# Up projections and gates: the high weights times both parts of the rows in one 512-column product, the halves added by VectorE

## The reference, cut to what matters

```python
# first block
proj = n @ w_in[l]                      # columns for q, k, v of two attentions, then the gates ga, gb
gate_a = sigmoid(ga + b_gate[l, :D_MODEL]);  gate_b = sigmoid(gb + b_gate[l, D_MODEL:])
h = h + (gate_a * ya + gate_b * yb) @ w_out[l]
...
u = n @ w_up                            # conv_gated_mlp: 1024 -> 2 * 2816, gate half and value half
u = causal_depthwise_conv3(u) + conv_b
h = h + (silu(u[..., :D_FF]) * u[..., D_FF:]) @ w_down
# second block, layer 0
x = x + (silu(h @ wg) * (h @ wu)) @ wd  # ffn_wg_2, ffn_wu_2: 1024 -> 2816 each
# second block, layer 1: top-2-of-8 expert SwiGLU, then a final rms_norm
```

## Time and profile before

| | |
|---|---|
| median of 3 runs | 1805.52 us (1805.26 to 1806.93) |
| the profiled execution, its own time | 1807.05 us |
| its span in the profile | 1805.3 us (25215 instructions) |
| PE busy | 1738.2 us (96%) |
| PE weight loads busy | 1425.7 us (79%) |
| DVE busy | 1184.4 us (66%) |
| ACT busy | 915.0 us (51%) |
| POOL busy | 55.9 us (3%) |
| DMA | 495.14 MB, mean 274 GB/s |
| chain that ended last | PE 81%, DVE 10%, ACT 6%, issue 2% |

### The profile page before, as it was taken

One profiled execution on the slowest core, in us unless ns is written; L12 is line 12 of the kernel. 1 busy time (PEld: TensorE's weight loads), 2 busy tenths in 40 slices (PEclk: granted clock), 3 DMA queues, 4 the chain that ended last, 5 costly groups with the idle time before them and its releaser, 6 DMA issues.

```text
span 1805.3 us, 25215 instructions
## 1 busy us (share of the span) xinstructions
PE 1738.2 (96%) x10391; PEld 1425.7 (79%) x10391; DVE 1184.4 (66%) x1517; ACT 915.0 (51%) x992; POOL 55.9 (3%) x71
## 2 busy tenths in 40 slices
PE   7999998999999999999999999999999999999997
PEld 7988897899998999998777777776776777676774
DVE  6664576766798665579677665665665665765653
ACT  5445655555564444345565553554455554554542
POOL 0000000000060000050000000000000000000000
PEclk9999999999999999999999999999999999999999
DMA  9423443565544365645669999999999999999996
GB/s 325 153 94 124 150 146 102 178 233 196 164 157 142 133 220 184 203 126 208 233 210 344 374 398 385 398 396 396 398 391 378 396 396 398 398 398 398 397 397 252
DMA packets 243562, 495.14 MB, mean 274 GB/s; under 512 B 9609, under 2 KB 99439, under 8 KB 229103
## 3 DMA queue, kind: packets, MB, share of 16 engines
q1 hardware_dynamic: 238927, 489.04, 74.0%
q10 hardware_dynamic: 4512, 4.40, 0.9%
HBM read 492.36 MB, written 1.05 MB: 273 GB/s over the span
## 4 chain that ended last, share of the span: by engine, by line
PE 81%; DVE 10%; ACT 6%; issue 2%; DMA 0%; ACTq 0%; DVEq 0%
PE bank L567 22%; PE bank L569 21%; PE bank L568 21%; DVE splitL L2159 6%; PE bank L1233 4%; PE bank L1266 4%; ACT splitH L1461 4%; PE bank L1212 1%; DVE co L2615 1%; PE bank L1168 1%; PE bank L1027 1%; PE bank L596 1%; PE bank L710 1%; PE bank L733 0%; PE bank L1085 0%
## 5 line engine op out<-in xcount | busy, mean ns | idle before, releaser
L2159 DVE TENSOR_TENSOR splitL<-raw,splitH 128x2048 fp32r<-128x2048 f32 (+1 forms) x248 | 561.8, 2273 | 155.3 <-ACT splitH L1461 154.5
L1461 ACT ACTIVATE splitH<-raw 128x2048 fp32r<-128x2048 f32 (+2 forms) x250 | 469.5, 1889 | 123.2 <-PE bank L569 102.4
L567 PE MATMUL bank<-RAH,splitH 128*128 128x256 f32 x1088 | 312.5, 287 | 6.0 <-DVE RAL L2169 3.3
L568 PE MATMUL bank<-RAL,splitH 128*128 128x256 f32 x1088 | 308.5, 284 | 0.0
L569 PE MATMUL bank<-RAH,splitL 128*128 128x256 f32 x1088 | 308.5, 284 | 0.0
L567 PE MATMUL bank<-splitH,RBH 128*128 128x512 f32 x736 | 293.5, 399 | 3.3 <-DVE splitL L2159 3.3
L569 PE MATMUL bank<-splitH,RBL 128*128 128x512 f32 x736 | 287.4, 391 | 0.0
L568 PE MATMUL bank<-splitL,RBH 128*128 128x512 f32 x736 | 286.9, 390 | 0.0
L2159 DVE TENSOR_TENSOR splitL<-rawx,splitH 128x2048 fp32r<-128x2048 f32 x89 | 203.2, 2290 | 28.7 <-ACT splitH L1461 28.2
L567 PEld LDWEIGHTS bank<-RAH,splitH 128*128 128x128 f32 x1088 | 209.3, 192 | 10.4 <-DVE RAL L2169 4.5
L568 PEld LDWEIGHTS bank<-RAL,splitH 128*128 128x128 f32 x1088 | 209.4, 192 | 1.0
(11 more groups left out here) (340 smaller groups left out, 2223.6 us busy)
## 6 DMA issues: line engine op xcount, KB each, us to landing
raw<-in_moe_wg SPq DMA_DIRECT2D x71, 1024.0 KB, 10.4
raw<-in_moe_wd SPq DMA_DIRECT2D x69, 1024.0 KB, 11.5
raw<-in_moe_wu SPq DMA_DIRECT2D x68, 1024.0 KB, 11.2
rawx<-in_moe_wu SPq DMA_DIRECT2D x44, 1024.0 KB, 11.6
rawx<-in_moe_wd SPq DMA_DIRECT2D x43, 1024.0 KB, 12.4
rawx<-in_moe_wg SPq DMA_DIRECT2D x41, 1024.0 KB, 11.8
raw<-in_w_in SPq DMA_DIRECT2D x24, 1024.0 KB, 6.2
raw<-in_w_up SPq DMA_DIRECT2D x22, 1024.0 KB, 5.1
```

Of the source, the lines that this page charges most:

```text
L567: e.matmul(o, lh, rh, start=start, stop=False)
L568: e.matmul(o, lh, rl, start=False, stop=False)
L1461: return e.activation(o, src, ACT.Copy)
L2159: e.tensor_tensor(l[:, 0:size], raws[home[n]][:, 0:size], h[:, 0:size].bitcast(F), ALU.subtract)\
```

## The change

`RAH` and `RAL` become the two halves of one tensor `RA`, so that a view `nA2` gives, for each chunk, 256 columns of high rows and 256 of low rows. A new helper `wstat2` makes a unit of the gates and of iterations 1 to 10 of both feed-forwards: for each chunk, one matmul of the high weights with all 512 columns, and one of the low weights with the 256 high columns. A bank then holds two halves, the left with high x high and low weights x high rows, the right with high weights x low rows. DVE adds them with a `tensor_reduce` over pairs, `both_halves`, from 512 columns of PSUM to 256 of SBUF. In the gates and in the second feed-forward `scaled` comes behind it and waits for it, and reads the sum from SBUF; in the first feed-forward the sum goes to `up`, ACT's and DVE's taps read it from there, and ACT's tap waits for the sum in place of PE. A bank is given back once its halves are added.

```diff
@@ -176,8 +176,8 @@
         diag = at("diag", [128, 31, 128], b0 + 64 * KB)
         b0 += 40 * KB
         X = at("X", [128, 2, 1024], b0)
-        RAH = at("RAH", [128, 2048], b0 + 8 * KB, FR)
-        RAL = at("RAL", [128, 2048], b0 + 16 * KB, FR)
+        RA = at("RA", [128, 4096], b0 + 8 * KB, FR)
+        RAH, RAL = RA[:, 0:2048], RA[:, 2048:4096]
         RBH = at("RBH", [128, 2048], b0 + 24 * KB, FR)
         RBL = at("RBL", [128, 2048], b0 + 32 * KB, FR)
         b0 += 40 * KB
@@ -192,6 +192,7 @@
             return v[:, :].rearrange("p (c n) -> p c n", c=8)
 
         nAH, nAL, nBH, nBL = k8(RAH), k8(RAL), k8(RBH), k8(RBL)
+        nA2 = RA[:, :].rearrange("p (s c n) -> p c s n", s=2, c=8)
 
 
         stage = at("stage", [128, 4, 128], ph + 72 * KB)
@@ -579,6 +580,24 @@
                              nL[:, b, :], start and q == 0, stop and q == len(kcs) - 1)
                 return mm
 
+            def wstat2(n, o, m, per=None):
+
+
+                H, Lo = pieces(n)
+                t.wait_ge(S.lo, cut(n))
+                o2 = o[:, :].rearrange("p (s n) -> p s n", s=2)
+                for k in range(8):
+                    if per:
+                        t.wait_ge(*per(k))
+                    h, l = H[:, k, m * 128:(m + 1) * 128], Lo[:, k, m * 128:(m + 1) * 128]
+                    if k == 0:
+                        e.matmul(o2, h, nA2[:, k, :, :], start=True, stop=False)
+                        e.matmul(o[:, 0:256], l, nAH[:, k, :], start=False, stop=False)
+                    else:
+                        e.matmul(o[:, 0:256], l, nAH[:, k, :], start=False, stop=False)
+                        mm = e.matmul(o2, h, nA2[:, k, :, :], start=False, stop=k == 7)
+                return mm
+
             def tstat(n, o, nH, nL, tb, kcs, cols, start, stop, per=None):
 
                 H, Lo = pieces(n)
@@ -793,8 +812,7 @@
                     for q, key in enumerate(("ga", "gb")):
                         for m in range(2):
                             b = bank["sg", 2 * s + m, q] = ring.take()
-                            wstat(slab[key][s], claim(b, (S.sg, 4 * s + 2 * q + m + 1))[:, 0:256], m, nAH, nAL, all8,
-                                  True, True).then_inc(S.prod, 1)
+                            wstat2(slab[key][s], claim(b, (S.sg, 4 * s + 2 * q + m + 1)), m).then_inc(S.prod, 1)
                         yield
 
             def branches():
@@ -931,7 +949,7 @@
                         bk = [ring.take() for _ in range(4)]
                         for u in range(4):
                             bank["gu", f, 0, u // 2, u % 2] = bk[u]
-                        first = 4 if f else 0
+                        first = 44 if f else 0
                         first_pair(up_g[0], st, bk[0:2], lambda m: (S.us, first + m + 1))
                         if f:
                             second_pair(up_v[0], st, bk[2:4], lambda m: (S.us, first + m + 3))
@@ -945,9 +963,8 @@
                             bk = [ring.take(), ring.take()]
                             for m in range(2):
                                 bank["gu", f, i, q, m] = bk[m]
-                                by = (S.us, 4 * i + 2 * q + m + 5) if f else (S.cv, 4 * (i - 1) + 2 * q + m + 1)
-                                wstat(n, claim(bk[m], by)[:, 0:256], m, nAH, nAL, all8, True, True,
-                                      normed).then_inc(S.prod, 1)
+                                by = (S.us, 44 * f + 4 * i + 2 * q + m + 1)
+                                wstat2(n, claim(bk[m], by), m, normed).then_inc(S.prod, 1)
                     if i > 0:
                         q = i - 1
                         hT = [v[:, 512 * (q % 4):512 * (q % 4) + 512].rearrange("p (m t) -> p m t", m=2)
@@ -1803,17 +1820,16 @@
                                 hi_to(n + (2 if i < 10 else 1))
                             if f == 0 and i > 0:
                                 for m in range(2):
-                                    a.wait_ge(S.prod, prod(n, m))
+                                    a.wait_ge(S.us, 4 * i + 2 * q + m + 1)
                                     if i > 1:
                                         a.wait_ge(S.h_lo, i - 1)
-                                    tap((G, V)[q][:, m, :], banks[bank["gu", f, i, q, m]][:, 0:256],
-                                        22 * q + 2 * i + m).then_inc(S.cv_a, 1)
+                                    tap((G, V)[q][:, m, :], up[q][m][:, :], 22 * q + 2 * i + m).then_inc(S.cv_a, 1)
                                 if q == 0:
                                     a.wait_ge(S.cv, 4 * (i - 1) + 2)
                                     e.activation(G[:, :, :], G[:, :, :], ACT.Silu).then_inc(S.cv_g, 1)
                             if f == 1 and q == 0:
                                 for m in range(2):
-                                    a.wait_ge(S.us, 4 * i + m + 5)
+                                    a.wait_ge(S.us, 44 + 4 * i + m + 1)
                                     if i > 1:
                                         a.wait_ge(S.h_lo, 11 + i - 1)
                                     e.activation(G[:, m, :], up[0][m][:, :], ACT.Silu).then_inc(S.cv_g, 1)
@@ -2208,6 +2224,9 @@
                     e.tensor_scalar(D[i][:, tb, :], ident, sm[:, slot + tb:slot + tb + 1], None, ALU.mult)\
                         .then_inc(S.diag, 1)
 
+            def both_halves(o, b):
+                return e.tensor_reduce(o, b[:, :].rearrange("p (s n) -> p n s", s=2), AX, ALU.add)
+
             def scaled(o, src, i):
                 v.wait_ge(S.R, i + 1)
                 return e.tensor_tensor(o, src, R[i][:, :], ALU.mult)
@@ -2372,7 +2391,9 @@
                             u = 2 * s + m
                             v.wait_ge(S.prod, prod(n, m))
                             v.wait_ge(S.av, 8)
-                            scaled(SG[:, u, q, :], banks[bank["sg", u, q]][:, 0:256], 0).then_inc(S.sg, 1)
+                            o = SG[:, u, q, :]
+                            v.wait_ge(S.step, step(both_halves(o, banks[bank["sg", u, q]])))
+                            scaled(o, o, 0).then_inc(S.sg, 1)
                         lo_to(n + 3)
                         yield
 
@@ -2538,10 +2559,14 @@
                         for q, n in enumerate((up_g[i], up_v[i])):
                             if i > 0:
                                 lo_to(n + (2 if i < 10 else 1))
+                            if f == 0 and i > 0:
+                                for m in range(2):
+                                    v.wait_ge(S.prod, prod(n, m))
+                                    both_halves(up[q][m][:, :], banks[bank["gu", f, i, q, m]]).then_inc(S.us, 1)
                             for m in range(2):
                                 if f == 0 and i == 0:
                                     break
-                                src = banks[bank["gu", f, i, q, m]][:, 0:256]
+                                src = up[q][m][:, :] if i > 0 else banks[bank["gu", f, i, q, m]][:, 0:256]
                                 if f == 0:
                                     o, ch, c = (G, V)[q][:, m, :], 22 * q + 2 * i + m, 4 * (i - 1) + 2 * q + m
                                     v.wait_ge(S.cv_a, c + 5)
@@ -2554,9 +2579,11 @@
                                     v.wait_ge(S.cv_g, 2 * i + 13)
                                 elif i > 1:
                                     v.wait_ge(S.h_hi, 11 + i - 1)
+                                if i > 0:
+                                    v.wait_ge(S.step, step(both_halves(src, banks[bank["gu", f, i, q, m]])))
                                 scaled(up[q][m][:, :], src, 5).then_inc(S.us, 1)
                                 if q:
-                                    v.wait_ge(S.us, 4 * i + 7 + m)
+                                    v.wait_ge(S.us, 44 + 4 * i + 3 + m)
                                     o = e.tensor_tensor(Y[:, m, :], G[:, m, :], up[1][m][:, :], ALU.mult)
                                     if m:
                                         o.then_inc(S.yf, 1)
```

## The result

| | before | after |
|---|---|---|
| median, runs of one comparison | 1806.24 us (1805.26 to 1807.5, 6 runs) | 1812.77 us (1812.09 to 1814.74, 6 runs) |
| ratio, 95% interval | | 1.0037 [1.0027, 1.0048] |
| profiled execution's own time | 1807.05 us | 1812.36 us |
| its span | 1805.3 us | 1810.6 us |

What follows compares the result with a forecast made beforehand. PE bounds the feed-forwards' middles; after the change DVE's own loop bounds the first. +6.3 (first feed-forward) - 1.4 (second) + 1.4 (gates) + 1.0 (clock) = +7.3, say +7 on 1805.52: 1812.5 us, own range 1808 to 1818, 1803 including rival 1.

Steps and rivals of the forecast that it cites:

- PE's gain: Gates and feed-forwards: 0.0119 us saved per matmul, 0.095 per unit, 9.1 us at most; iterations need 16.60 us of PE.
- The two starts named as a sign: In the changed kernel's profile, PE's matmuls would start 0.228 and 0.120 us apart.
- The reduction: DVE's added reductions would take 0.69 us each, 0.60 back to back, priced by elements read.
- figure for cheap reductions: First feed-forward: with reductions of 0.35 us each, DVE's loop is 15.8 us, DVE catches up, a tail of 1 remains.
- The first feed-forward: DVE's loop grows from 14.17 to 16.89 us, so DVE never catches up and the stage ends 6.3 us later.
- The clock at that end: Before the last down slab PE idles about 5 us and the clock falls; DVE's chain hides the cost.
- The second feed-forward: PE stays the bound and gains 3.6 us; DVE's chain at the end adds 2.2; net -1.4 us.
- The gates: BL comes 1.55 us later, PE wins back 0.57 with the last three slabs; net +1.4 us, between -1.5 and +4.
- 1.0 for the clock: Gates: a slower granted clock after PE's longer idle time costs 1.0 us, between 0 and 2.5.
- Rival 1: DVE keeps up in the first feed-forward, which takes -1.4; total -1.4, about 1804 us; chance 0.17.
- Rival 2: PE's gain arrives whole because a pair reduction costs 0.35 us or less: 1798 us; chance 0.11.
- Rival 3: Each matmul gone saves only the skill's 2.5 ns: 1816 us with the clock; chance 0.04.

Runs made afterwards that it cites:

- short_sum: Changed kernel with half the elements summed in the first feed-forward and adjacent pairs summed in the gates: 1810.94 us in one execution, first feed-forward 199.55 us.
- three_mm: Changed kernel with its reductions kept but three 256-column matmuls per chunk again: median 1816.23 us, ratio to before 1.0059.
- silu_late: Changed kernel with ACT's high copy moved ahead of the Silu in first feed-forward iterations 1 to 10: median 1806.73 us, ratio to before 0.9999.
- early_mix: Kernel before with new units only in iterations 1 to 7 of the first feed-forward and 1 to 9 of the second: median 1805.49 us, ratio 0.9994.
- first_only: Kernel before with the change in the first feed-forward alone: median 1813.79 us, ratio to before 1.0040.
- best_b: Kernel before with new units in both feed-forwards' iterations 1 to 9 and the last three gate slabs, high copy ahead of Silu: 1800.74 us, ratio 0.9971.
- gates_only: Kernel before with the change in the gates alone, both feed-forwards as before: median 1808.65 us, ratio to before 1.0015.

## Why the prediction was right

Forecast 1812.5, measured 1812.77; 0.37% slower. By its own steps:

1. **PE's gain.** Forecast 0.095 us per unit, 16.60 us per iteration; measured 0.088 and 16.63. Every matmul that is gone gives 0.011 us, not 0.0119. Over 96 units that is 0.7 us less. The two starts named as a sign, 0.228 and 0.120 us apart, did not come one by one: they are 0.234 and 0.116 in the second feed-forward of the changed kernel, and only their sum, 0.350, is near the 0.348.
2. **The reduction**, 0.69: measured 0.683, and back to back 0.60. `short_sum` and the row of two results bear out the rule behind it, the elements read. Wrong was the figure for cheap reductions, a loop of 15.8 us at 0.35 each: it leaves out ACT's tap. By the path that `short_sum` shows it would be 14.17 + 2 x (0.35 + 0.68) = 16.2, an estimate. The forecast itself was not touched, as with 0.69 both ways of adding give 2.72 per loop.
3. **The first feed-forward**, +6.3: measured +6.52, with a loop of 16.90 (forecast 16.89) and the last low part at 497.43 (497.5). The times can be compared as they stand, since the stage starts only 0.14 us earlier than before: the later gates and the quicker cross attention nearly cancel. `three_mm` (DVE's part alone gives the same stage) and `silu_late` (2 us out of the loop, and the stage 9.2 shorter) show that this loop is the cause. One sentence was wrong: "PE hardly stalls until the end, as the slabs are split ahead of it". PE stalls 2.30 us before iteration 2 and is held at 16.90 from then on; only 4.71 us are left as idle time at the end. It changed nothing in this sum, because DVE's chain sets the end, but in `early_mix` it did.
4. **The clock at that end** fell as expected, and DVE's chain hid most of it, as I said. Stretches of 5 us of the changed kernel:

```profile
495.00:500.00 5.00, 1.82 (x4) 1.49 (x5) 3.13 (x6) 3.23 (x3) 0.00 (x0) 0.71 0.64 172
500.00:505.00 5.00, 5.00 (x15) 3.78 (x14) 4.92 (x4) 1.64 (x4) 0.00 (x0) 0.60 0.44 123
```

DVE's first two additions to X end at 504.92, and PE, busy with the slow down slab, goes on to the transposes at 505.08 with no wait. In `first_only` DVE was the later one by 0.22 us. That two chains came out within 0.2 us of each other I had not worked out.

5. **The second feed-forward**, -1.4: measured -1.25. The chain from the last gate unit to X takes 786.82 - 771.12 = 15.70 us against 13.56, 2.14 more, where 2.2 was forecast. PE comes to that unit 3.16 us earlier in the stage (forecast 3.6), and before, DVE was done 0.28 us ahead of PE's transposes, a room that takes 0.23 of the longer chain and stood in no term: -3.16 + 2.14 - 0.23 = -1.25. DVE's work of 8.8 us per iteration was read from a window that cuts iterations; by whole ones it is 9.72, which still leaves PE the bound. DVE's timeline of after, and PE's transposes, which now wait for it:

```profile
771.12 0.69 DVE L2228 TENSOR_REDUCE up<-bank 128x256 f32<-128x512 f32 x1 [1.63 <-PE bank L598]
...
786.82 1.87 DVE L2440 TENSOR_TENSOR X<-X,bank 128x512 f32<-128x512 f32 x3
```

```profile
788.15 1.09 PE L615 MATMUL bank<-cb,X 128*128 128x128 f32 x8 [1.95 <-DVE X L2440]
```

6. **The gates**, +1.4, and 1.0 for the clock: the wait for BL grew by 1.53, to 2.96 and not to the 3.9 of the forecast, against the earlier trace rows, and the matmul behind it came 1.36 later (forecast 1.55):

```profile
197.85 0.91 PE L793 MATMUL bank<-BL,c 128*128 128x384 f32 x2 [2.96 <-DVE BL L2382]
...
220.67 0.66 PE L803 MATMUL bank<-PT,vB 128*64 128x256 f32 x4 [0.29 <-ACT PT L1643]
```

The 0.57 that the last three slabs were to win back came to 0.10 at the second row, as PE waits for ACT there, and the hold that `best_b` shows for `yTL` takes 0.27 behind it: 1.36 - 0.10 + 0.27 = 1.53. So a smaller delay and a smaller gain made up for each other, and +1.4 was near by chance. The stage ended 1.53 later with the clock at 1.00 and 2.36 later in `gates_only`, where it fell: 0.8 us for it, and not in every execution.

7. **Cross attention** stood in no term. The same code took 42.61 us in the profiled execution of before, where the clock fell, and 40.94 here, where it did not:

```profile
275.00:280.00 5.00, 2.97 (x18) 2.41 (x17) 2.76 (x8) 1.02 (x4) 0.00 (x0) 1.00 0.36 127
280.00:285.00 5.00, 3.50 (x18) 2.49 (x18) 2.72 (x11) 3.29 (x11) 0.00 (x0) 1.00 0.00 0
```

That is why the spans differ by 5.3 us and the stages that the change touches by 1.53 + 6.52 - 1.25 = 6.8. The medians say 6.5, and forecast was 7.3 with the clock at the gates, 6.3 without it. So part of the close agreement with the median is chance. The change costs 6.5 us where 7.3 was worked out and 7 forecast; the 0.3 us between 1812.5 and 1812.77 are so few because the kernel before took 1806.24 us in this comparison, 0.7 more than the 1805.52 that the forecast was added to. And the clock term of 1.0 did not show in the profiled execution.

Rival 1 (DVE keeps up) needed a loop shorter by 0.3 us, but its price was wrong: in `short_sum` the loop is 0.5 us shorter, below PE's, and the stage still takes 1.5 us more than before (part of it the clock's), not 1.4 less. With the 14.88 of `silu_late` DVE does catch up early. Rival 2 fell with the price of the reduction. Rival 3 fell with iterations of 16.63 us.

## What to carry to other kernels

Before work is moved from the busiest engine to another, work out that engine's own loop with its idle time in it: DVE was busy 26.5 us of 40, yet its loop had only 2.4 us to give, since 2.5 of its idle time stood in a dependence and not at a wait for PE. Where such a loop becomes the longer one, look first for the idle time inside it; here one copy moved on ACT gave back more than the change cost, 2.0 us of it without the change. To see what the change itself is then worth, compare it with the kernel before that has the same copy moved. Count such a loop by its longest path of waits, not by the sum of the new instructions: halving a reduction took 0.27 us out per pair, not per reduction. And apply a small gain per unit only where the receiver has room, not in the units whose results end a stage.
